# Two transformer blocks on one core: whole weight loads, warm-up matmuls and narrower attention units

## The reference, cut to what matters

```python
# first_block: two layers
for i in range(2):
    h = rmsnorm(x, norm_mix[i])
    if i == 0:                       # "fox": 12 heads of 64, causal, with a decay
        p = h @ fox_w_in             # 1024 x (3*768 + 12 + 256)
        o_mix = fox_mixer(p[..., :-256], ...)
    else:                            # "mla": low-rank q and kv, rope, 12 heads of 96
        p = h @ mla_w_in             # 1024 x (256 + 128 + 32 + 256)
        o_mix = mla_mixer(p[..., :-256], ...)
    o_mem = memory_cross(p[..., -256:], k_mem, v_mem, ...)    # 4 heads, 256 keys
    x = x + concat(o_mix, o_mem) @ w_out[i]
    x = x + conv_ffn(rmsnorm(x, norm_ffn[i]), w_up, conv_w, conv_b, w_down)   # width 2816
# second_block: one layer
x = x + 0.5 * swiglu(rms_norm(x, g_ffn1), ...)
# local attention (8 query heads, window 128, sinks), a 31-tap convolution, memory attention
x = x + concat(y_attn, y_conv, y_mem) @ w_out_2
x = x + 0.5 * swiglu(rms_norm(x, g_ffn2), ...)
```

## Time and profile before

| what | value |
|---|---|
| device time, median of 3 runs | 2083.71 us (2083.41 to 2084.61) |
| the profiled execution: its own time | 2083.41 us |
| its span, first to last instruction | 2081.6 us |
| granted clock, mean over the span | 0.999 of full |
| TensorE busy | 2055.7 us, 99% of the span |
| VectorE busy | 1280.0 us, 61% |
| ScalarE busy | 962.2 us, 46% |
| bytes moved | 185.53 MB |

### The profile page before, as it was taken

How to read it: one execution, slowest core, us unless ns; L and a number is a source line. 1 busy time by engine, 2 the same in 40 slices (tenths; PEclk the granted TensorE clock), 3 DMA queues, 4 the chain that set the end, 5 groups by cost and what they waited for, 6 DMA issues and landing times.

```text
span 2081.6 us, 29983 instructions
## 1 busy us (share of the span) xinstructions
PE 2055.7 (99%) x11114; PEld 1730.2 (83%) x11114; DVE 1280.0 (61%) x2086; ACT 962.2 (46%) x1880; POOL 50.5 (2%) x95
## 2 busy tenths in 40 slices
PE   7999999999999899999999999999999999999999
PEld 7999888888889788888888888888889778888887
DVE  7655677637754787875577544344548985544442
ACT  7755554424445875543344433223344664322331
POOL 0000001000000110000000000000001100000000
PEclk9999999999999999999999999999999999999999
DMA  6222233333332011333333333333332123333332
GB/s 206 80 63 61 62 93 100 97 96 97 97 94 87 19 46 55 98 97 96 97 98 100 97 95 98 97 96 97 96 96 72 37 77 96 96 97 96 97 97 90
DMA packets 101666, 185.53 MB, mean 89 GB/s; under 512 B 11408, under 2 KB 14864, under 8 KB 101264
## 3 DMA queue, kind: packets, MB, share of 16 engines
q1 hardware_dynamic: 101520, 183.61, 30.2%
HBM read 181.47 MB, written 2.10 MB: 88 GB/s over the span
## 4 chain that ended last, share of the span: by engine, by line
PE 92%; DVE 4%; ACT 2%; issue 1%; SPq 0%; DMA 0%; DVEq 0%; ACTq 0%
PE PSA L1905 25%; PE PSA L1907 25%; PE PSA L1906 25%; PE PSA L1923 3%; PE PSA L1925 3%; PE PSA L1924 3%; PE PSA L2037 2%; PE PSA L2023 2%; PE PSA L2011 1%; DVE PSTAT L2176 1%; ACT PP L2422 1%; PE PSA L1965 1%; DVE RS L2068 1%; DVE WL L2080 0%; PE PSA L2004 0%
## 5 line engine op out<-in xcount | busy, mean ns | idle before, releaser
L2352 ACT ACTIVATE WH<-RAW 128x512 fp32r<-128x512 f32 (+3 forms) x681 | 426.7, 627 | 811.0 <-PE PSA L1907 693.5
L2080 DVE TENSOR_TENSOR WL<-RAW,WH 128x512 fp32r<-128x512 f32 (+3 forms) x681 | 469.4, 690 | 398.4 <-ACT WH L2352 376.6
L1905 PE MATMUL PSA<-HNh,WH 128*128 128x512 f32 x1440 | 562.4, 391 | 0.0
L1907 PE MATMUL PSA<-HNh,WL 128*128 128x512 f32 x1440 | 560.3, 389 | 0.0
L1906 PE MATMUL PSA<-HNl,WH 128*128 128x512 f32 x1440 | 560.2, 389 | 0.0
L1906 PEld LDWEIGHTS PSA<-HNl,WH 128*128 128x128 f32 x1440 | 270.3, 188 | 57.2 <-issue 1.2
L1905 PEld LDWEIGHTS PSA<-HNh,WH 128*128 128x128 f32 x1440 | 270.3, 188 | 56.9 <-issue 1.2
L1907 PEld LDWEIGHTS PSA<-HNh,WL 128*128 128x128 f32 x1440 | 270.3, 188 | 56.3
L1905 PE MATMUL PSA<-Gh,WH 128*128 128x512 f32 x704 | 273.9, 389 | 0.0
L1906 PE MATMUL PSA<-Gl,WH 128*128 128x512 f32 x704 | 273.9, 389 | 0.0
L1907 PE MATMUL PSA<-Gh,WL 128*128 128x512 f32 x704 | 273.9, 389 | 0.0
(11 more groups left out here) (252 smaller groups left out, 2244.9 us busy)
## 6 DMA issues: line engine op xcount, KB each, us to landing
RAW<-in_w SPq DMA_DIRECT2D x659, 256.0 KB, 2.6
XT<-in_x SPq DMA_DIRECT2D x8, 256.0 KB, 5.0
MT<-in_mem SPq DMA_DIRECT2D x2, 1024.0 KB, 6.1
out_x<-XT SPq DMA_DIRECT2D x8, 256.0 KB, 2.1
RAW<-in_w SPq DMA_DIRECT2D x8, 208.0 KB, 2.4
RAW<-in_w SPq DMA_DIRECT2D x6, 192.0 KB, 2.3
RAW<-in_w SPq DMA_DIRECT2D x8, 134.0 KB, 5.2
PAR<-in_par SPq DMA_DIRECT2D x1, 207.0 KB, 6.0
```

The source lines that it names most:

```text
L1905: pe.matmul(out, wh, xh, start=(a["start"] and c == 0), stop=False)
L1907: p = pe.matmul(out, wl, xh, start=False, stop=ends)
L2080: dve.tensor_tensor(l, r, h, ALU.subtract).then_inc(done.sem("split.dve"), 1)
L2352: act.activation(h, r, ACT.Copy).then_inc(done.sem("split.act"), 1)
```

## The change

Six things change together:

1. `unit_cols` and `unit_slice` go. Every unit is loaded, rounded and split in its full 512 columns, in all 22 units that were narrower.
2. A table `WARM` names six steps. When such a step is written, and if some bank of PSUM that no step holds has been free for at least four beats of the list, a `warm` step is put ahead of it: 9, 13, 5, 10, 14 or 12 matmuls of 384 columns in bfloat16 on constants, into that bank, whose result nobody reads. The keys are (attention, job, unit): attention 0 is fox, 1 is mla, 2 is the local mixer. There are 63 such matmuls in all: 22 in fox, 29 in mla, 12 in the local mixer.
3. The six causal jobs of mla get `limit=128`: four units (128, 256, 384, 512) where there were three.
4. The four local jobs and the two memory jobs beside them get `limit=256`: four units (128, 256, 256, 256 and 4 x 256) where there were two.
5. These six jobs get `spare = True`, which also alters the assumed lags: exponentials are written 0.8 beats after the maxima, and the closing steps in another order.
6. In the planner the second term of TensorE's choice is 0.0 where it was the place in the queue (`n + PASSES * ...`, with `PASSES` 0).

```diff
+WARM = {("pbcast", (0, 1)): 9, ("pscore", (0, 2, 0)): 13,
+        ("pscore", (1, 0, 0)): 5, ("pscore", (1, 0, 1)): 10, ("pturn", (1, 0, 0, 0)): 14, ("pscore", (2, 0, 0)): 12}
...
-                        z = (clock[e] + late, shaping(e, i) if late else n + PASSES * bool(shaping(e, i)), e, self.first[e, i], i, t)
+                        z = (clock[e] + late, shaping(e, i) if late else 0.0, e, self.first[e, i], i, t)
...
         def step(kind, key, **a):
+            if (kind, key) in WARM:
+                warm((kind, key), WARM[kind, key])
...
+        def warm(key, n):
+            banks = [b for b in pick(8, range(8)) if ready(psum.freed[b], 4)]
+            if banks:
+                psum.take(("warm", key), [], banks[0])
+                step("warm", key, n=n, bank=banks[0])
...
-                             VG[p // 2 % 2][:, :, 128 * (p % 2):128 * (p % 2) + 128], CAUSAL, p, pair_got[p], lag=1, wants=5))
+                             VG[p // 2 % 2][:, :, 128 * (p % 2):128 * (p % 2) + 128], CAUSAL, p, pair_got[p], lag=1, wants=5, limit=128))
...
-                     VB[:, :, :], tiles, n, pair_got[n], sink=(n, 4 + n), wants=3) for n in range(4)]
+                     VB[:, :, :], tiles, n, pair_got[n], sink=(n, 4 + n), wants=3, limit=256) for n in range(4)]
...
-        jobs += mem_pairs(1, 6, [], QR[:, 2, :], roots_of["mq", 1280])
+        jobs += mem_pairs(1, 6, [], QR[:, 2, :], roots_of["mq", 1280], 256)
...
+        for j in jobs:
+            j.spare = True
...
+                elif k == "warm":
+                    w.wait_ge(s_cb, 16)
+                    for t in psum.before["warm", key]:
+                        w.wait_ge(*done(*t))
+                    for _ in range(a["n"]):
+                        pe.matmul(PS[a["bank"]][:, 0:384], IDB, CB[:, 0:384], start=True, stop=True)
...
-                    sp.dma_start(RAW[u % NRAW][:, unit_slice[u]], io["w"][u][:, unit_slice[u]]).then_inc(s_raw[u % NRAW], 16)
+                    sp.dma_start(RAW[u % NRAW][:, :], io["w"][u]).then_inc(s_raw[u % NRAW], 16)
```

More of the change, by code:

```diff
@@ L130, in weight_plan @@
     return t
[L134 to L139, removed]
 PARAMS = [("mix0", 8), ("mix1", 8), ("nf0", 8), ("nf1", 8), ("memn", 8), ("f1", 8), ("mix2", 8), ("memn2", 8),
@@ L279 @@
 SHAPING = 0.18
-PASSES = 0
 PATIENT = ("pe",)
@@ L395, in run @@
                 found = None
-                for n, i in enumerate(todo[e][:reach]):
+                for i in todo[e][:reach]:
                     t = open_at(self.first[e, i])
@@ L560 @@
     "lnlow": ("lnlow.dve",),
+    "warm": (),
     "tables": (),
@@ L575, in program @@
         n_units = (len(plan) + UT - 1) // UT
-        unit_slice = [slice(0, unit_cols(plan, u)) for u in range(n_units)]
         CB = sb("CB", [128, 384], BF16)
@@ L2073, in vector @@
                 if k == "split":
-                    c = unit_slice[key]
-                    r, h, l = (x[:, c] for x in (RAW[key % NRAW], WH[key % NSPL], WL[key % NSPL]))
+                    r, h, l = RAW[key % NRAW], WH[key % NSPL], WL[key % NSPL]
                     w.wait_ge(s_raw[key % NRAW], 16 * (key // NRAW + 1))
@@ L2079, in vector @@
                         w.wait_ge(*done("unit", key - NSPL))
-                    dve.tensor_tensor(l, r, h, ALU.subtract).then_inc(done.sem("split.dve"), 1)
+                    dve.tensor_tensor(l[:, :], r[:, :], h[:, :], ALU.subtract).then_inc(done.sem("split.dve"), 1)
                 elif k == "plow":
@@ L2346, in scalar @@
                 if k == "split":
-                    r, h = (x[:, unit_slice[key]] for x in (RAW[key % NRAW], WH[key % NSPL]))
+                    r, h = RAW[key % NRAW], WH[key % NSPL]
                     w.wait_ge(s_raw[key % NRAW], 16 * (key // NRAW + 1))
@@ L2351, in scalar @@
                         w.wait_ge(*done("split.dve", key - NSPL))
-                    act.activation(h, r, ACT.Copy).then_inc(done.sem("split.act"), 1)
+                    act.activation(h[:, :], r[:, :], ACT.Copy).then_inc(done.sem("split.act"), 1)
                 elif k == "part":
@@ L2596, in sync @@
                 if c % 2 == 0:
-                    sp.dma_start(RAW[c // 2][:, unit_slice[c // 2]], io["w"][c // 2][:, unit_slice[c // 2]]).then_inc(s_raw[c // 2], 16)
+                    sp.dma_start(RAW[c // 2][:, :], io["w"][c // 2]).then_inc(s_raw[c // 2], 16)
                 sp.dma_start(XT[:, c, :], io["x"][:, c, :]).then_inc(s_x[c], 16)
@@ L2601, in sync @@
             for u in range(KC // 2, NRAW):
-                sp.dma_start(RAW[u][:, unit_slice[u]], io["w"][u][:, unit_slice[u]]).then_inc(s_raw[u], 16)
+                sp.dma_start(RAW[u][:, :], io["w"][u]).then_inc(s_raw[u], 16)
             sp.dma_start(TRI, io["tri"]).then_inc(s_tri, 16)
```

## The result

The changed kernel takes 2096.12 us (median of four runs, 2095.74 to 2096.54), the kernel before 2084.16 us beside it (2083.41 to 2085.65): a ratio of 1.0056, 95% interval 1.0044 to 1.0068. It is 12.0 us slower. The forecast was slower by 6.8 us, 2090.2 us, in a range from 2084.0 to 2098.0. Sign and range held; the size is nearly twice what I gave, just outside the forecast case's own range (2086.0 to 2096.0).

The account below looks back on a forecast made before the run. TensorE, busy 2055.7 of 2081.6 us, was taken as the bound, with VectorE also full in the local mixer. Terms 2.2 + 0.5 + 3.7 + 0.3 + 1.0 + 1.1 - 2.0 = 6.8 us gave 2090.2 us, range 2084.0 to 2098.0.

Parts of the forecast that it names:

- forecast case: Whole kernel: the summed forecast of 2090.2 us, given chance 0.62 and its own range of 2086.0 to 2096.0 us.
- planner's term: Planner's choice for TensorE: the changed second term alters nothing, 0.0 us.
- full units, start and mla: Start: 2.2 us, of which 1.8 from a later DMA landing of unit 4; mla mixer: 0.5 us for grown units.
- 22 warm matmuls in fox: Fox mixer: no TensorE hole, so all lie on the path at 0.167 us each, 3.7 us slower.
- 29 in mla: Mla mixer: 4.8 us of warm matmuls mostly fill holes and keep the clock full, net 0.3 us slower.
- mla in four units: Mla mixer: one more copy on VectorE and ScalarE for each of six jobs, 1.1 us slower.
- 12 warm matmuls, local: Local mixer: 2.0 us of TensorE ahead of the first scores, half counted, 1.0 us slower.
- part 6: Local mixer, 24 finer units with one copy: VectorE loses 3.5 us, ScalarE gains 6.7; taken as -2.0 us, faster.
- rival with ScalarE: Local mixer: ScalarE's 6.7 us of copies come on the path; 15.5 us slower, 2098.9 us, chance 0.10.
- rival of hidden room: Fox mixer: the 22 warm matmuls slip into hidden TensorE gaps; 3.1 us slower in all, 2086.5 us, chance 0.08.
- rival of steps that are not written: Mixers: no free bank, so no warm matmuls are written; 1.8 us slower, 2085.2 us, chance 0.12.
- faster case: Mla and local mixers: held by hand-overs, finer units remove the holes; -7.1 us, 2076.3 us, chance 0.08.

Follow-up runs that it names:

- experiment 1: Kernel before with the fox jobs' causal mask matmuls moved between the scores' second and third pass, 30 more changes of kind: 2089.19 us beside 2084.04, 5.2 us slower.
- experiment 2: Kernel before with the four local jobs' mask matmuls moved between their passes, 31 more changes of kind: 2086.38 us beside 2083.74, 2.6 us slower.
- experiment 3: Kernel before with the local mixer's limit of 256 and spare alone, no warm matmuls: 2090.81 us beside 2084.04, 6.8 us slower.
- experiment 4: Kernel before with the finer local units, spare and the 12 warm matmuls of the local mixer: 2088.96 us beside 2083.74, 5.2 us slower.
- experiment 9: Kernel before with the 29 warm matmuls of mla alone: 2083.95 us beside 2083.57, 0.4 us slower, ratio 1.0001.
- experiment 6: Changed kernel with limit and spare of the six local and memory jobs undone: 2090.54 us, 6.5 us slower than the kernel before at 2084.04.
- experiment 10: Kernel before with full 512-column units alone: 2085.25 us beside 2083.57, 1.7 us slower, ratio 1.0007.
- experiment 11: Kernel before with the mla jobs in four units alone: 2085.17 us beside 2083.57, 1.6 us slower, ratio 1.0008.

## Why the prediction was right in sign and short in size

| term | forecast, us | measured alone, us |
|---|---|---|
| planner's term | 0.0 | same instructions |
| full units, start and mla | 2.2 + 0.5 | 1.7 |
| 22 warm matmuls in fox | 3.7 | 4.4 (3.8 by the profile) |
| 29 in mla | 0.3 | 0.4 |
| mla in four units | 1.1 | 1.6 |
| 12 warm matmuls, local | 1.0 | -1.6, on finer units (about 0 on coarse ones) |
| finer local units with one copy | -2.0 | 6.8 |
| sum | 6.8 | 13.3; together 12.0 |

The sum is 5.2 us short. The term that was mis-sized is part 6, 8.8 us off by itself (-2.0 where 6.8 was measured). It took net 3.5 us off VectorE, and counted TensorE's work as unchanged. That the time still lies in the range is partly luck: no case inside the range had such a term, and the 12 local warm matmuls (2.6 us better than forecast) and the parts together (12.0 where they add up to 13.3) took some of the error back. Three things stood against part 6.

- *VectorE did not get lighter.* I priced 24 units with joint maxima; eight had separate banks, and the 7.6 us of copies came back as 7.7 us of maxima and their small steps. The trace of before already had a hint in the earlier trace rows: one unit of eight was split in two.
- *TensorE did not stay the same.* Half as large units nearly double the changes of kind (43 to 78). They cost 0.17 us each in fox (experiment 1) and 0.08 in the local mixer (experiment 2), 2.6 us here. The prediction had no term for it, though the kernel's own planner can be told of such a cost (`PASSES`).
- *The clock, likely.* With finer units the granted clock fell to half for some microseconds; the version with the 12 warm matmuls kept it and was 1.6 us faster, by medians whose intervals overlap.

2.6 and 1.6 leave 2.6 of the 6.8 us without a shown cause, and adding them up takes the pieces as independent. The rows say where to look: TensorE is busy longer, and waits less. ScalarE's longer copies are hardly it: matmuls wait 0.6 us for them in the changed kernel and in experiment 3, and weight loads 3.2 us in the changed kernel, where they waited 2.5 us for VectorE's copies before. Weight loads wait 2.9 us more for exponentials, part of it hidden behind matmuls in flight; hand-overs of twice as many units may be the rest, and no run separates them.

My rival with ScalarE gave 15.5 us, nearer to 12.0 than my 6.8, and its 6.7 us for this part is what was measured (6.8). That is a coincidence of numbers: it needs TensorE to stand waiting for the copies, and the traces have 0.6 us of that.

On the warm matmuls the reasons held best. Where TensorE has no hole they are paid in full, so the rival of hidden room falls. Where holes and a dip of the clock are, 4.8 us of them cost 0.4: what the Trainium skill says in "TensorE: Matmul & The Clock Gate" (Part 1: The HAM clock gate), that activity releases the throttle, agrees with the granted clock in experiments 4 and 9 (1.00 where the kernel before had 0.96 and experiment 3 had 0.50). In the local mixer I expected a cost of 1.0: it was nothing ahead of coarse units (experiment 6), and a likely gain ahead of finer ones. The guard found a bank at all six places, so the rival of steps that are not written falls too.

The start was priced too high by holding GB/s fixed. Around the landing of unit 4 the rate rose from 351 to 381 GB/s, and 1.0 us was left of my 1.8. Whether the 0.5 for the grown units in the mla mixer was right isn't shown: the 0.7 us of experiment 10 there are within that stretch's own variation. Three small slips in the sums change nothing: the longer rounding and remainder are 0.47 us together, not 0.4; the straight line gives 0.17 us for each engine's copies, so 2.1 and not 1.9 us; and the chance of no measurable change adds up to 0.23.

The faster case, mixers held by hand-overs, didn't come true where it was tried: in experiment 3 halving the units took the local stretch's holes from 5.4 to 4.3 us and made it 7.9 us longer. In the mla mixer the 1.6 us of experiment 11 are not clear of zero.

## What to carry to other kernels

Before making units smaller, count what each unit brings with it whatever its size: the changes between kinds of matmul on the busiest engine, the small steps on the second busiest, and what depends on buffers being neighbours. Filling a hole is worth something only where the hole is; matmuls that nobody reads cost their full length in a stage without holes (fox) and almost nothing where they fill holes (mla, and the local mixer with coarse units). A transfer with short rows may save less than its bytes say: look at how its GB/s compares with that of full rows.

## What was not expected of the hardware

- In the fox mixer, moving bfloat16 masks on the full array in between float32 scores on 64 rows, 30 more changes of kind with the same matmuls, cost 5.2 us, 0.17 each.
- The granted clock falls to 0.50 somewhere between 682 and 714 us in all eleven profiled kernels without the 29 warm matmuls of mla, and stays at 1.00 in the three with them.
- 63 idle matmuls, 10.5 us of TensorE, made the changed kernel only 2.0 us longer.
- From 14 to 17 us, loads of rows of 2048 bytes ran at 381 GB/s (378 with full units alone) where a mix with rows of 1072 bytes ran at 351.
